# Two transformer blocks on one core: the inverse square roots of the norms taken by one power step on GpSimd

## The reference, cut to what matters

```python
def _rms(x, w=None):
    y = x * lax.rsqrt(jnp.mean(x * x, axis=-1, keepdims=True) + 1e-6)
    return y if w is None else y * w

# first block: differential attention and bidirectional retention
xn = _rms(x, norm_w);  qa, ka, va, ga, qr, kr, vr, gr = split(xn @ w_in)
qa, ka = _rms(qa per head of 64, q_norm_w), _rms(ka per head of 64, k_norm_w)
oa = _rms(diff_attention(qa, ka, va), subln_w) * 0.8      # 4 heads of 128
orr = _rms(bidirectional_retention(qr, kr, vr))           # 4 heads of 128
x = x + concat([oa * silu(ga), orr * silu(gr)]) @ w_out
# second block: convolution branch and sliding-window attention
h = _rms(x, norm_g);  v_c, b_c, c_c, z_c, q, k, v, z_a, gate = split(h @ w_in_2)
q, k = _rms(q per head of 64), _rms(k per head of 64)     # 16 and 4 heads
x = x + (sigmoid(gate_a) * y_a + sigmoid(gate_b) * y_b) @ w_out_2
```

## Time and profile before

| | |
|---|---|
| median of three runs | 814.98 us |
| span of the profiled execution, first to last instruction | 811.6 us |
| PE busy | 805.4 us (99%) |
| DVE busy | 634.0 us (78%), 1112 instructions |
| ACT busy | 339.9 us (42%) |
| POOL busy | 187.8 us (23%), 189 instructions |
| granted TensorE clock, mean | 0.999 |

### The profile page before, as it was taken

How to read it: one execution, slowest core, us unless ns; L and a number is a source line. 1 busy time by engine, 2 the same in 40 slices (tenths; PEclk the granted TensorE clock), 3 DMA queues, 4 the chain that set the end, 5 groups by cost and what they waited for, 6 DMA issues and landing times.

```text
span 811.6 us, 11794 instructions
## 1 busy us (share of the span) xinstructions
PE 805.4 (99%) x4364; PEld 691.4 (85%) x4364; DVE 634.0 (78%) x1112; ACT 339.9 (42%) x721; POOL 187.8 (23%) x189
## 2 busy tenths in 40 slices
PE   9999999999999999999999999999999999999998
PEld 7788888888888888888888888888889988999986
DVE  5998778768984476885578788978798678599998
ACT  4374465632122254342545544551134222455580
POOL 2222111111121221122324555544260114000000
PEclk9999999999999999999999999999999999999999
DMA  7236644445143322336868677596935634866562
GB/s 241 88 96 233 233 155 156 151 161 182 53 156 114 95 78 78 90 93 130 177 144 163 140 151 161 131 182 135 202 104 183 182 98 135 235 184 183 184 203 78
DMA packets 132862, 120.47 MB, mean 148 GB/s; under 512 B 4749, under 2 KB 100550, under 8 KB 132806
## 3 DMA queue, kind: packets, MB, share of 16 engines
q1 hardware_dynamic: 124326, 102.94, 40.9%
q0 software_dynamic: 8448, 16.78, 12.4%
q10 hardware_dynamic: 32, 0.01, 0.0%
HBM read 117.62 MB, written 35.65 MB: 189 GB/s over the span
## 4 chain that ended last, share of the span: by engine, by line
PE 92%; DVE 5%; issue 1%; ACT 1%; DMA 1%; POOL 0%; DVEq 0%; ACTq 0%
PE proj L1886 23%; PE proj L1888 23%; PE proj L1887 23%; PE bank_t L1900 3%; PE bank_o L1975 2%; DVE x L1592 1%; PE score L1888 1%; PE score L1887 1%; PE score L1886 1%; DVE w_lo L1247 1%; PE score L2050 1%; PE score L1960 1%; PE score L1961 1%; PE score L2049 1%; PE bank_o L2068 1%
## 5 line engine op out<-in xcount | busy, mean ns | idle before, releaser
L1247 DVE TENSOR_TENSOR w_lo<-w_raw,w_hi 128x1024 fp32r<-128x1024 f32 x151 | 192.0, 1274 | 44.3 <-POOL w_hi L778 36.1
L778 POOL TENSOR_SCALAR w_hi<-w_raw 128x1024 fp32r<-128x1024 f32 x101 | 118.6, 1174 | 438.6 <-DMA w_raw<-in_w_in_dram 314.6
L1886 PE MATMUL proj<-xt_hi,w_hi 128*128 128x512 f32 (+1 forms) x448 | 171.2, 382 | 0.0
L1888 PE MATMUL proj<-xt_hi,w_lo 128*128 128x512 f32 (+1 forms) x448 | 168.1, 375 | 0.0
L1887 PE MATMUL proj<-xt_lo,w_hi 128*128 128x512 f32 (+1 forms) x448 | 167.8, 374 | 0.0
L1888 PEld LDWEIGHTS proj<-xt_hi,w_lo 128*128 128x128 f32 x448 | 84.4, 188 | 15.6
L1887 PEld LDWEIGHTS proj<-xt_lo,w_hi 128*128 128x128 f32 x448 | 84.5, 189 | 14.1
L1886 PEld LDWEIGHTS proj<-xt_hi,w_hi 128*128 128x128 f32 x448 | 84.5, 189 | 14.0
L1886 PE MATMUL proj<-w_hi,xt_hi 128*128 128x512 f32 x152 | 60.9, 401 | 0.2 <-ACT prob L1012 0.2
L1888 PE MATMUL proj<-w_hi,xt_lo 128*128 128x512 f32 x152 | 59.5, 391 | 0.0
L1887 PE MATMUL proj<-w_lo,xt_hi 128*128 128x512 f32 x152 | 59.4, 391 | 0.0
(11 more groups left out here) (471 smaller groups left out, 1871.2 us busy)
## 6 DMA issues: line engine op xcount, KB each, us to landing
w_raw<-in_w_in_dram SPq DMA_DIRECT2D x79, 512.0 KB, 3.8
w_sums<-in_w_in_dram SPq DMA_DIRECT2D x8, 1024.0 KB, 7.0
w_sums<-w_sums POOLq DMA_DIRECT2D x8, 1024.0 KB, 9.1
w_raw<-w_sums SPq DMA_DIRECT2D x16, 512.0 KB, 3.8
w_raw<-w_sums SPq DMA_DIRECT2D x32, 256.0 KB, 3.3
w_raw<-in_w_out_dram SPq DMA_DIRECT2D x14, 512.0 KB, 3.3
w_raw<-in_w_in_dram SPq DMA_DIRECT2D x26, 256.0 KB, 3.3
w_sums<-in_w_attn_out_dram SPq DMA_DIRECT2D x4, 1024.0 KB, 6.5
```

What stands on the lines that cost most here:

```text
L778: pool.tensor_scalar(hi, raw, 1.0, 1.0, ALU.mult, ALU.mult).then_inc(hi_done, 1)
L1247: dve.tensor_tensor(lo, raw, hi.bitcast(F32), ALU.subtract).then_inc(w_split, 1)
L1886: pe.matmul(out, left[0], right[0], start=first, stop=False)
L1888: return pe.matmul(out, left[1], right[0], start=False, stop=last)
```

## The change: what it does

In `rsqrt`, DVE keeps the first of the twelve instructions (scale and add) and then waits for POOL. POOL raises the same numbers to the power -0.5 with one instruction on two inputs (`rs_v` and a constant tile of -0.5, filled at the start). POOL goes through the twelve roots in the order in which DVE asks for them (`ROOTS`); in its order each stands at the same half piece as on DVE, behind the rounding that this half may begin with and ahead of its other steps.

```diff
-RSQRT_SEED = 0x5F3759DF
+def roots_after(n, half):
+    steps = [(4, D) for kind, m in STEPS[(n, half)] if kind == "RS_X"]
+    steps += [(16, P) for kind, m in STEPS[(n, half)] if (kind, m) == ("AN", DA_HEADS - 1)]
+    steps += [(4, P) for kind, m in STEPS[(n, half)] if kind == "RB"]
+    tiles = [(16 if u == U_KV else 32, HD) for u in (U_K, U_Q, U_KV, U_Q20, U_Q21) if (n, half) == (4 * u + 3, 1)]
+    return tiles + steps
+
+ROOTS = [(n, half, count, width) for n in range(PIECES) for half in range(2) for count, width in roots_after(n, half)]
...
+            pool.memset(minus_half[:], -0.5).then_inc(pool_chain, 1)
             pool.iota(table[:, 0, :].bitcast(I32), pattern=[[1, TAB]], base=-CENTRE, channel_multiplier=-1).then_inc(setup, 1)
...
+            def take_root(i):
+                width = ROOTS[i][2]
+                if i == 0:
+                    pool.wait_ge(pool_chain, 2)
+                pool.wait_ge(sums_ready, i + 1)
+                pool.tensor_tensor(rs_y[:, 0:width], rs_v[:, 0:width], minus_half[:, 0:width], ALU.pow).then_inc(roots_done, 1)
...
                         for m in ROUNDED_AT.get(n, ()):
                             if not AOUT <= m < COUT:
                                 round_piece(m)
+                    for i, root in enumerate(ROOTS):
+                        if root[0:2] == (n, half):
+                            take_root(i)
...
             def rsqrt(n, width):
-                v, y, t = rs_v[:, 0:n], rs_y[:, 0:n], rs_t[:, 0:n]
-                done(dve.tensor_scalar(v, v, 1.0 / width, EPS, ALU.mult, ALU.add))
-                done(dve.tensor_scalar(t.bitcast(I32), v.bitcast(I32), 1, None, ALU.logical_shift_right))
-                done(dve.tensor_scalar(y.bitcast(I32), t.bitcast(I32), -1.0, float(RSQRT_SEED), ALU.mult, ALU.add))
-                for _ in range(3):
-                    done(dve.scalar_tensor_tensor(out=t, in0=y, scalar=-0.5, in1=y, op0=ALU.mult, op1=ALU.mult))
-                    done(dve.tensor_tensor(t, t, v, ALU.mult))
-                    done(dve.scalar_tensor_tensor(out=y, in0=t, scalar=1.5, in1=y, op0=ALU.add, op1=ALU.mult))
+                assert ROOTS[roots[0]][2:] == (n, width)
+                roots[0] += 1
+                dve.tensor_scalar(rs_v[:, 0:n], rs_v[:, 0:n], 1.0 / width, EPS, ALU.mult, ALU.add).then_inc(sums_ready, 1)
+                dve.wait_ge(roots_done, roots[0])
```

More of the change, by code:

```diff
@@ L326, in build @@
         ssq = sb("ssq", [P, 4]); ssq_half = sb("ssq_half", [P, 4, 2])
-        rs_v = sb("rs_v", [P, 32]); rs_y = sb("rs_y", [P, 32]); rs_t = sb("rs_t", [P, 32])
+        rs_v = sb("rs_v", [P, 32]); rs_y = sb("rs_y", [P, 32]); minus_half = sb("minus_half", [P, 32])
         mx2 = sb("mx2", [P, 4, 4]); neg_m2 = sb("neg_m2", [P, 4, 4]); sink_m = sb("sink_m", [P, 4, 4])
@@ L587, in build @@
         ssq_done = sem("ssq_done")
-        rs_done = sem("rs_done")
+        rs_done = sem("rs_done"); sums_ready = sem("sums_ready"); roots_done = sem("roots_done")
         diag_done = sem("diag_done"); rs_turned = sem("rs_turned"); rs_row_done = sem("rs_row_done")
@@ L765, in prepare_mask @@
                 pool.memset(mask[:], 0.0).then_inc(pool_chain, 1)
-                pool.wait_ge(pool_chain, 2)
+                pool.wait_ge(pool_chain, 3)
                 pool.affine_select(out=mask[:], in_=mask[:], compare_op=ALU.is_ge, fill=BIG, base=P,
                                    pattern=[[-1, 2 * P]], channel_multiplier=1).then_inc(pool_chain, 1)
-                pool.wait_ge(pool_chain, 3)
+                pool.wait_ge(pool_chain, 4)
                 pool.affine_select(out=mask[:], in_=mask[:], compare_op=ALU.is_ge, fill=BIG, base=-1,
@@ L1219, in done @@
                 dve.wait_ge(dve_chain, chain[0])
+            roots = [0]
             def rsqrt(n, width):
-                v, y, t = rs_v[:, 0:n], rs_y[:, 0:n], rs_t[:, 0:n]
-                done(dve.tensor_scalar(v, v, 1.0 / width, EPS, ALU.mult, ALU.add))
-                done(dve.tensor_scalar(t.bitcast(I32), v.bitcast(I32), 1, None, ALU.logical_shift_right))
-                done(dve.tensor_scalar(y.bitcast(I32), t.bitcast(I32), -1.0, float(RSQRT_SEED), ALU.mult, ALU.add))
-                for _ in range(3):
-                    done(dve.scalar_tensor_tensor(out=t, in0=y, scalar=-0.5, in1=y, op0=ALU.mult, op1=ALU.mult))
-                    done(dve.tensor_tensor(t, t, v, ALU.mult))
-                    done(dve.scalar_tensor_tensor(out=y, in0=t, scalar=1.5, in1=y, op0=ALU.add, op1=ALU.mult))
+                assert ROOTS[roots[0]][2:] == (n, width)
+                roots[0] += 1
+                dve.tensor_scalar(rs_v[:, 0:n], rs_v[:, 0:n], 1.0 / width, EPS, ALU.mult, ALU.add).then_inc(sums_ready, 1)
+                dve.wait_ge(roots_done, roots[0])
             def take_xt_low(m):
```

## The result

The changed kernel takes 834.57 us (four runs, 832.66 to 835.63) against 815.14 us; the ratio is 1.023, 95% interval 1.0199 to 1.0261. I had forecast 815.3 us in a range of 814.2 to 821.0: wrong. The case that came true is rival 2, for which I had worked out 835 us and given a chance of 0.12. The profiled execution has a span of 830.8 us against 811.6.

A forecast was written before the change was run, and what follows sets the result against it. TensorE, busy almost throughout the stretch with the roots, was taken to bound the kernel; +0.2 to +0.3 us, mainly 0.25 us lost at the q unit, on 814.98 gave 815.3 us, range 814.2 to 821.0.

The forecast's parts named there:

- rival 2: Power as slow library routine, 7.4 us at width 32; TensorE late at multiplied tiles, 20 us lost, 835 us; chance 0.12.
- what comes: Twelve powers on GpSimd, each estimated at 1.55 us for width 32, 0.8 for 16, 0.3 for 4.
- The upper bound of 3.27 us: Power of 32 elements on GpSimd costs at most a whole ordinary two-input instruction of 1024 elements, 3.27 us.
- the sum: Over all twelve roots: loss 0.25 us at one place, nothing at eleven, gain 0 to 0.1 us.
- What bounds the kernel: TensorE sets the end, busy 345.57 of 346.00 us around the roots; sparing VectorE buys at most 0.43 us.
- The rooms: Time a width-32 root may take before TensorE loses: 1.2 to 1.3 us at q unit, 2.2 at k unit.
- A rounding moved behind the root meets the multiplies: At the q unit, GpSimd's moved rounding lengthens VectorE's four multiplies by 1.05 us; two roundings met, 2.10 us.
- VectorE's busy time: Sign in the changed profile: VectorE's busy time down by about 28 us.
- rival 3: Only the first root's power is dear, 6 us for code not yet there; loss 2.5 to 3 us, 818 us; chance 0.07.
- The page's per-element figures: Skill's GpSimd cycles per element, about 12 with data-dependent branches, give 0.3 us for 32 elements: power nearly free.

The follow-up runs named there:

- The half power: The changed kernel with the power taken of only 16 columns at the four roots of width 32, the other 16 holding 0.1: 819.94 us, ratio 1.0053.
- the parts apart: The changed kernel with each power split into column parts, taken as soon as their sums are there: 823.11 us; mended in two places, 818.99 us.
- the power twice: The changed kernel with each power taken twice, once into a tile that nobody reads: 864.25 us, ratio 1.061.

## Why the prediction was wrong

The step that failed is in "what comes": the price of the power. I took 45 ns for each column and 0.1 us for the instruction, 1.55 us at width 32. It is 158 ns and 0.39 us: 5.45, 2.91 and 1.02 us at widths 32, 16 and 4. The upper bound of 3.27 us was no bound. It was the duration of an instruction of 1024 additions, and that a power of 32 numbers should stay under it was a guess dressed as a row: nothing in the trace tied the two operations together. With such an operation the honest upper end was rival 2's (7.4 us), and its chance of 0.12 was too small. With the measured price the other steps of the sum give a loss of 4.2 us at the q unit, in place of the 0.25 that I had put there.

- **What bounds the kernel; VectorE freed brings nothing.** Right. With the widths at which the power is short, VectorE is spared and the ratio is 1.0002.
- **The rooms.** Right at four places, wrong at one. Price less room, with the rooms written before (the 2.7 and the 5.4 below are those that rival 2's terms imply), gives 5.45 - 1.25 = 4.2 us at the q unit (measured 4.3), 5.45 - 2.2 = 3.25 at the k unit (3.1), 5.45 - 2.7 = 2.75 at the second block's first q unit (2.5). The half power confirmed the first two at another price. For the attention heads I had counted 2.5 us in rival 2 at 3.7 us, a room of 1.2, which gives 1.7 us at 2.91; they lost 1.5. At the second block's second q unit rival 2 had a loss of 2 us at 7.4, a room of 5.4, and so none at 5.45; the two waits there are 2.2 us.
- **A rounding moved behind the root meets the multiplies.** Right, and one short: three roundings, not two, stood behind the longer power (3.94 us in a row at 74.33), and the multiplies took 2.52 us more than undisturbed. With a short operation in the power's place the moved roundings cost nothing measurable.
- **VectorE's busy time.** The sign named was a fall by about 28 us; it fell by 17.8. The 28.73 us of the Newton rounds went, but what now meets GpSimd's roundings became longer.
- **The first power is dear (rival 3).** Refuted. The first takes 1.04 us, the others of its width 1.02, and the work behind it is earlier than behind the Newton rounds: the diagonal that stood at 23.69 stands at 23.27. The Trainium skill (GPSIMD Engine Reference, 2.1 Instruction dispatch) has about 6 us for the first call of freshly loaded code; nothing of this shows here, so the power doesn't behave as such a call.
- **The page's per-element figures.** From the Trainium skill (GPSIMD Engine Reference, 3.1 Elementwise), with its figure for data-dependent branching, I had estimated 0.3 us for the power at width 32; measured are 5.45 us. The multiplication at the same width took 0.255 us.
- **Rival 2** had the mechanism and the places right, and its 835 us against the measured 834.57 is luck, by offsetting errors: it supposed 7.4 us and 20 us of waits; the power costs 5.45, the waits are 13.7 us, and 5.5 us are longer busy time, of which 3.2 at the halved clock. No step of mine had the clock in it.

## What to carry to other kernels

An operation for which the trace has no row can't be bounded by a row of another operation on the same engine. If its duration decides the sign, say so and spread the range to the price at which the forecast turns; here the rooms gave that point (about 2.5 us at width 32). Work moved off an engine that nobody waits for brings nothing, and it costs as soon as the mover must wait for the answer: ask what the waiting engine did in that time and who needs it next. A wait put into an in-order queue also holds what stands behind it, and what is held comes in one burst afterwards.

## What the runs showed of the hardware that I had not expected

- A power on GpSimd costs 0.39 us and 158 ns for each column of 128 partitions (1022, 2914 and 5446 ns at 4, 16 and 32); a multiplication of the same tiles 202 to 255 ns.
- A power and VectorE meet in another way than a rounding and VectorE do. With the parts apart, the multiply of VectorE at 40.04 (two inputs, 128x512) began 0.07 us after the second power of width 8 and passed beside it in 0.69 us; the one at 44.84 met a rounding, which began at 44.78, and took 1.52 us. But the power at 138.60 above, which began 0.05 us after a two-input instruction of VectorE, took 2.05 us in place of 1.02.
- Tiles that lie 128 bytes further in each partition of SBUF made the matmuls of this kernel slower by 4.2 us in sum, ratio 1.0037 (1.0024 to 1.0049), and by 4.2 to 4.4 us in two more kernels with such a tile. Whoever adds a scratch tile to an experiment measures that too.
- In all these traces, behind their first 15 us, TensorE has 24 unfilled pauses of 1.9 to 9.6 us, and at 18 of them the granted clock was 0.5 for 3.4, 6.8 or 10.2 us; of the six that last 1.9 to 2.0 us it was so at four, and once not at 3.1 us. At none of the shorter pauses was it so. With the power twice (pauses up to 9.6 us) the mean clock was 0.977. That pauses are the only occasion isn't shown: one execution of the kernel before (824.97 us) had a mean clock of 0.995, and no trace of it is kept.
